# Attention steps of a two-block kernel: the weighing of values and the next projection's products regrouped by two

## The reference, cut to what matters

```
sc = einsum("bnqhd,bknjhd->bhnqkj", q_r, k_r) * scale
sc = where(mask, sc + bias, NEG)
p  = softmax(sc)
o  = einsum("bhnqkj,bknjhd->bnqhd", p, v_r)
```

## Time and profile before

| what | value |
|---|---|
| median of 3 runs | 2443.91 us |
| the 3 runs | 2440.36, 2443.91, 2445.88 us |
| the profiled execution's own time | 2440.27 us |
| its span in the profile | 2438.4 us |
| granted clock of PE, mean | 0.997 |
| PE busy | 2409.4 us, 99% |
| DVE, POOL, ACT busy | 77%, 56%, 38% |
| chain that ended last | PE 86%, DVE 7%, POOL, ACT and issue 2% each |
| PE busy from 1190 to 1440 us, where the pairs lie | 248.78 of 250 us |

### The profile page before, as it was taken

The page is one execution under the profiler, slowest core; times in us unless marked ns, Lnnn a source line. Parts: engine busy times, 40 slices in busy tenths (PEclk is TensorE's granted clock), DMA queues, the critical chain, the costliest instruction groups (busy, mean ns, idle before and its releaser), DMA issues.

```text
span 2438.4 us, 37303 instructions
## 1 busy us (share of the span) xinstructions
PE 2409.4 (99%) x13817; PEld 1978.4 (81%) x13817; DVE 1875.5 (77%) x1904; ACT 937.0 (38%) x1288; POOL 1361.0 (56%) x789
## 2 busy tenths in 40 slices
PE   8999999999999999999999999999999999999998
PEld 8788887888888788887777778888888888887886
DVE  6755555776666788888877789354799999999998
ACT  5333335353333533314233331310355445443433
POOL 3322222269887767772322223333379999978785
PEclk9999999999999999999999999999999999999999
DMA  6111112334444755431311111113222222235342
GB/s 226 36 37 41 34 34 92 108 119 151 153 155 166 262 167 160 150 125 39 127 41 33 40 35 52 44 48 126 95 87 78 86 91 81 77 132 179 104 122 81
DMA packets 243637, 244.79 MB, mean 100 GB/s; under 512 B 16944, under 2 KB 212187, under 8 KB 238811
## 3 DMA queue, kind: packets, MB, share of 16 engines
q1 hardware_dynamic: 214484, 165.13, 21.9%
q10 hardware_dynamic: 29062, 78.44, 8.4%
HBM read 181.13 MB, written 64.17 MB: 101 GB/s over the span
## 4 chain that ended last, share of the span: by engine, by line
PE 86%; DVE 7%; POOL 2%; issue 2%; ACT 2%; DMA 1%; SPq 0%; DVEq 0%; ACTq 0%; POOLq 0%
PE psum L1414 30%; PE psum L1703 26%; PE psum L1823 11%; PE psum L2069 7%; PE psum L1972 3%; PE psum L1452 2%; PE psum L1538 1%; PE psum L1904 1%; PE psum L1477 1%; PE psum L1885 1%; DVE sq_sum_gain L3474 0%; POOL ffn_s_lo L1283 0%; PE psum L1598 0%; DVE h_lo L2949 0%; DVE sq_sum L3231 0%
## 5 line engine op out<-in xcount | busy, mean ns | idle before, releaser
L1226 POOL CAST w_hi<-w_raw 128x1024 fp32r<-128x1024 f32 x85 | 100.4, 1181 | 773.8 <-issue 375.2
L1414 PE MATMUL psum<-h_hi,w_hi 128*128 128x512 f32 x1040 | 333.4, 402 | 1.5 <-DVE h_lo L3052 1.3
L1414 PE MATMUL psum<-h_lo,w_hi 128*128 128x512 f32 x1040 | 321.9, 391 | 0.0
L1414 PE MATMUL psum<-h_hi,w_lo 128*128 128x512 f32 x1040 | 320.8, 390 | 0.0
L1414 PEld LDWEIGHTS psum<-h_hi,w_lo 128*128 128x128 f32 x1040 | 195.5, 188 | 42.0
L1414 PEld LDWEIGHTS psum<-h_lo,w_hi 128*128 128x128 f32 x1040 | 195.5, 188 | 41.7
L1234 POOL TENSOR_TENSOR w_lo<-w_raw,w_hi 128x1024 fp32r<-128x1024 f32 x85 | 222.7, 2620 | 9.9 <-DVE h_lo L2949 3.2
L1414 PEld LDWEIGHTS psum<-h_hi,w_hi 128*128 128x128 f32 x1040 | 189.5, 188 | 42.9 <-issue 7.3
L3528 DVE SCALAR_TENSOR_TENSOR conv_t<-u_t,cols,conv_t 128x1024 f32<-128x1024 f32 x120 | 179.8, 1498 | 2.4
L1283 POOL TENSOR_TENSOR ffn_s_lo<-ffn_s_sum,ffn_s_hi 128x512 fp32r<-128x512 f32 x84 | 159.8, 1932 | 7.0 <-POOL ffn_s_sum L1269 4.1
L1703 PE MATMUL psum<-ffn_t_hi,ffn_s_hi 128*128 128x512 f32 x252 | 98.0, 389 | 0.0
(11 more groups left out here) (605 smaller groups left out, 6808.3 us busy)
## 6 DMA issues: line engine op xcount, KB each, us to landing
w_raw<-in_w_in SPq DMA_DIRECT2D x120, 256.0 KB, 3.0
w_raw<-in_w_up SPq DMA_DIRECT2D x76, 256.0 KB, 3.4
act_parts<-act_mixed ACTq DMA_DIRECT2D x15, 1024.0 KB, 3.8
down_part_raw<-act_parts SPq DMA_DIRECT2D x14, 1024.0 KB, 5.4
down_part_raw<-act_parts SPq DMA_DIRECT2D x15, 768.0 KB, 6.4
ffn_raw<-in_w_up SPq DMA_DIRECT2D x44, 256.0 KB, 3.4
ffn_rows<-ffn_gate ACTq DMA_DIRECT2D x22, 512.0 KB, 2.6
ffn_part_raw<-ffn_rows SPq DMA_DIRECT2D x18, 512.0 KB, 4.7
```

Source lines behind the costliest of these rows:

```text
L1226: pool.tensor_copy(hi, raw).then_inc(weight_hi, 1)
L1414: last = pe.matmul(psum[:, first_bank + t, :], w, a[:, k, t * HALF:(t + 1) * HALF], start=(k == order[0] and j == 0), stop=(k == order[-1] ...
```

## The change

The fourth projection's feature tiles no longer follow steps 1 to 8 one by one. Two of them, P(k) and P(k+1), stand together in each of the steps 2, 4, 6 and 8. The weighing of values is done in every other step, for two groups: step 4 has W(0) and W(1), step 6 W(2) and W(3), step 8 W(4) and W(5), step 10 W(6) and W(7). The steps 1, 3, 5, 7 have S(g) and T(g-1) alone, and step 1 also Tv. The wait for `v_tiles_ready` moves from step 3 to step 4. Since the transposed weights of two groups are now held while a third is copied, `prob_t` gets a third buffer of 3 KB a partition (`prob_t_third`, behind `u_t` in the arena), and the index is `g % 3`. Nothing is computed otherwise, and the number of matmuls, copies and transfers is the same.

```diff
-NEXT_AFTER = {k + 1: [k] for k in range(KT)}
+NEXT_AFTER = {k + 2: [k, k + 1] for k in range(0, KT, 2)}
...
+            ("prob_t_third", [P, 2, WIN], F32))
+        prob_t_slots = [prob_t[:, 0, :, :], prob_t[:, 1, :, :], prob_t_third[:, :, :]]
...
                         pe.matmul(psum[head, g // 4, (g % 4) * P:(g % 4 + 1) * P], v_keys[:, first + c, head],
-                                  prob_t[:, g % 2, j, c * P:(c + 1) * P], start=(c == 0), stop=(c == n - 1))
+                                  prob_t_slots[g % 3][:, j, c * P:(c + 1) * P], start=(c == 0), stop=(c == n - 1))
...
                 for g in range(1, GROUPS + 3):
-                    if g == 3:
+                    if g == 4:
                         pe.wait_ge(v_tiles_ready, p + 1)
-                    if g >= 3:
+                    if g >= 4 and g % 2 == 0:
+                        weigh_values(p, g - 4)
                         weigh_values(p, g - 3)
...
-                        act.activation(prob_t[:, g % 2, j, 0:n], psum[:, 6 + j, 0:n], ACT.Copy).then_inc(prob_t_ready, 1)
+                        act.activation(prob_t_slots[g % 3][:, j, 0:n], psum[:, 6 + j, 0:n], ACT.Copy).then_inc(prob_t_ready, 1)
```

More of the change, by code:

```diff
@@ L502, in two_blocks @@
         U_PAD = CONV_PAD + SEQ + CONV_PAD
-        (sig_cb, q_hi, q_lo, k_hi, k_lo, v_t, v_keys, bias_raw, prob_t, bias, near_mask, prob, qk32, u_t) = arena(
+        (sig_cb, q_hi, q_lo, k_hi, k_lo, v_t, v_keys, bias_raw, prob_t, bias, near_mask, prob, qk32, u_t,
+         prob_t_third) = arena(
             ("sig_cb", [P, CT, SEQ], F32), ("q_hi", [P, SEQ], F32R), ("q_lo", [P, SEQ], F32R),
@@ L508, in two_blocks @@
             ("bias", [P, 2, 5, P], F32), ("near_mask", [P, 3, P], F32), ("prob", [P, 2, 2, WIN], F32),
-            ("qk32", [P, SEQ], F32), ("u_t", [P, 2, U_PAD], F32))
+            ("qk32", [P, SEQ], F32), ("u_t", [P, 2, U_PAD], F32),
+            ("prob_t_third", [P, 2, WIN], F32))
+        prob_t_slots = [prob_t[:, 0, :, :], prob_t[:, 1, :, :], prob_t_third[:, :, :]]
         inv_spread, inv_wide = qk32, v_t
```

## The result

The changed kernel takes 2445.93 us in the median of 22 runs (2443.17 to 2447.72), the kernel before 2440.97 in the median of 22 (2438.51 to 2445.88). The medians lie 4.96 us apart. The ratio put on record is 1.0015, with a 95% interval of 1.0009 to 1.0021: 3.7 us slower (2.2 to 5.1), where +4.2 was forecast. The forecast's 2448.1 stands 2.2 us too high, since it was built on a median of three runs that lay 2.9 us above that of 22.

What follows compares the result with a forecast made beforehand. PE, busy nearly throughout, was taken as the bound; per pair 0.73 us of blocks plus 0.32 of waits gave 1.05, over four pairs 4.2, added to 2443.91 for 2448.1 us; range 2442.0 to 2452.5.

Steps and rivals of the forecast that it cites:

- The cover: Steps 1 and 2: T(1) starts as before, about 1.2 us idle replaces P(0), whose 1.36 us must be done later.
- P: Behind T(1), seven lone product blocks (10.85 us) become four double ones of 2.91 (11.64): +0.79 us a pair.
- W: Behind T(1), seven weighing blocks become four, each block saved worth 0.14 us: -0.42 us a pair.
- T ahead of W: Steps 4, 6, 8: transposes now followed by weighing cost 0.12 us more each, bounds 0 to 0.14: +0.36 a pair.
- T on ACT: Even steps, waits for ACT's copies: T(5) free by 0.26 us, T(3) none or 0.02, T(7) 0.3.
- The sum: Over a pair, 0.73 us of blocks plus 0.32 of waits: 1.05 us, four pairs 4.2 us slower.
- some 9 us of listed waits: In the pairs, PE's waits were to rise from 1.2 us to some 9.
- Rival 1: Even steps: ACT's copies land some 0.3 us later, about 0.6 more a pair, 6.6 in all, 2450.5 us; chance 0.26.
- Rivals 2 to 4: In the pairs: T(1) earlier, 2442.3 us, or everything hidden (0.10 together); passages costing more than block lengths show, 2438.3 us (0.04).
- the signs of being wrong: In the changed profile: T(1) moves up, T(3) or T(5) wait 0.2 us or more, or a double P under 2.8.
- the 0.2% that I had called no change: Whole kernel: a measurement tells about 0.2%, 4.9 us, from no change; chance of same 0.59, slower 0.36, faster 0.05.

Runs made afterwards that it cites:

- e1: The change with P(0) back alone in step 1 and P(1) alone in step 2; pairs 224.55 us, ratio 1.0005.
- e2: The change with products still paired in even steps but values weighed one group a step as before; median 2453.59 us, ratio 1.0053.
- e3: The change with values still weighed for two groups but products one a step as before; pairs 223.77 us, ratio 1.0003.
- e4: Against the change: products one a step, values weighed two groups at once in steps 5 and 7, singly in 3, 8, 9, 10; ratio 0.9994.
- e5: The change with DVE's convolution tap after group 0 taken to the end of the pair; pairs 223.27 us, ratio 0.9995.
- e6: The order of the kernel before, with the third buffer, DVE's tap after group 0 at the pair's end; pairs 221.74 us, ratio 0.9992.
- e7: The change with both regroupings one step earlier, paired products in steps 3, 5, 7 and paired values in 5, 7, 9; pairs 220.57 us, ratio 0.9983.
- e8: e7 with DVE's tap after group 0 taken to the end of the pair; median 2440.65 us, ratio 0.9995.
- e9: e8 with the four pairs' taps counted 21, 21, 20, 20 in place of 20, 20, 22, 20; median 2436.99 us, ratio 0.9982.
- e10: The same file as e7, timed again together with e9; pairs 220.50 us, ratio 0.9992.

## Why the prediction was right

All at once, the pairs against those of before (us); expected from block lengths, measured in one profile each:

| kernel | expected | measured | ratio |
|---|---|---|---|
| the change | +4.2 | +4.78 | 1.0015 |
| e1, P(0) back | +1.4 | +1.49 | 1.0005 |
| e2, products alone | +12 | +12.16 | 1.0053 |
| e3, values alone | +0.8 | +0.71 | 1.0003 |
| e4, values in odd steps | -1.1 | -0.97 | 0.9994 |
| e5, change, tap later | 0.0 | +0.21 | 0.9995 |
| e6, before, tap later | -1.4 | -1.32 | 0.9992 |
| e7, both odd | -1.8 | -2.49 | 0.9983 |
| e8, both odd, tap later | -3.2 or -1.8 | +0.14 | 0.9995 |
| e9, e8 with even taps | -3.8 | -3.85 | 0.9982 |
| e10, e7 again | -2.5 | -2.56 | 0.9992 |

- **The cover.** T(1) stayed at 4.75 us behind S(1), and the idle time appeared where P(0) was: 0.26 ahead of Tv and, of the 1.2 foretold ahead of S(2), 1.05 as listed and 1.17 start to start. e1 and e5 show the cause from both ends: with P(0) back the loss shrinks, with DVE's tap gone it does too.
- **P.** 2.94 for a double one, 2.91 was reckoned: 11.75 us a pair for four, and not 11.64. The seven lone ones of before were read too short as well, 10.91 in all and not 10.85, so the term is +0.84 in place of +0.79.
- **W.** 1.46 for 24, as reckoned; the term is -0.45 in place of -0.42.
- **T ahead of W.** 0.80 or 0.81 against 0.63, so 0.18 and not the 0.12 taken from Tv, and above my upper bound of 0.14: another +0.17 a pair. The bound was wrong because I read the passage's price from other pairs of neighbours. That it costs at all agrees with the Trainium skill's sentence on drains at a change of tiling mode (TensorEngine Tiling (Array Packing), Key Properties).
- **T on ACT.** T(3) and T(5) did not wait, as forecast. T(7) lost 0.20 us (0.07 and 0.13) in three pairs where I had 0.3; the later T, by its dearer passages, met a copy that was nearer. In the fourth pair it lost 0.56: DVE began the scores of group 7 1.16 us behind S(7) (1426.48 to 1427.64) and not 0.81. It does so in the kernel before as well (1420.80 to 1421.96), where P(6) stood ahead of T(7) and hid it; I had read the first pair only. Why DVE is later there was not tried.
- **The sum.** 1.12 us from T(1) to the block of 20 in three pairs, 1.05 forecast: 0.84 for P, -0.45 for W, 0.53 for T ahead of W and 0.20 of waits. The passage was 0.17 too cheap and the waits 0.12 too dear, so part of the nearness is luck. The fourth pair, 1.44, was not foreseen. The list of waits was off more: I foretold some 9 us of listed waits, the profile lists 5.8, since the one ahead of Tv and the short ones of T(7) are not in it and S(2) of the second pair waits only 0.58.
- **The rivals.** Rival 1 (ACT late in all even steps) did not come in the change, but e2 is what it looks like when one W less stands there. Rivals 2 to 4 would have needed T(1) to move or blocks to be worth more; neither was seen. Of the signs of being wrong (T(1) earlier, T(3) or T(5) late by 0.2, a double P below 2.8) none came.
- **The level.** +0.15% fell inside the 0.2% that I had called no change, as forecast, and was told from zero only by 22 runs a side.

## What to carry to other kernels

Work of a busy engine that stands in front of a point set by other engines is free there, as long as it fits in, and costs its full length anywhere else; before moving it, check whether the next wait would come at the same time without it. Regrouping saves the passages between kinds of work, here 0.14 us for a W block and 0.2 for a P block; it pays only in an order that keeps each distance from a producer to its consumer (here 3.4 us from S(g) to T(g)) filled, and shifting the grouping by one step, with P(0), P(1), W(0) and W(7) left single, turned +4.8 us into -2.5. After that, look for the engine whose list sets the point itself: moving one tap of DVE was worth 4.6 us in the change and 1.3 in the order of before, and 1.3 on top of e7 once DVE's list had room for it (e9); without that room it lost 2.6 (e8).

## What was not expected of the hardware

- A passage has a price that depends on both neighbours: eight transposes take 0.85 us ahead of a 128x128 product and 0.97 ahead of a 64x128 one (in e6 too, where DVE's maximum for S(2) is there 1.29 us early, so that it is no hidden wait), six take 0.63 ahead of a product and 0.81 ahead of a 128x64 one.
- A wait of PE of 2.34 us was followed, 1.6 us after its end, by some 3.5 us at the lower clock (granted 0.60 from 1398 to 1402 us) and 1.55 us more went there than in the other pairs. In the changed kernel waits of 1.05 us, three times, and of 0.58 once did nothing of the kind: the granted clock is 1.00 over the six microseconds that hold each of them and what follows it.
- DVE's tap of 128x1024 takes 1.2 us start to start, but some that lie beside POOL's `w_lo` take far longer: one of 3.42 us at 1388.32 in the kernel before, 0.07 behind the start of a `w_lo` of 2.40 us, and at the end of the third pair four took 5.86 us in e6 and 7.87 in e8. What decides which is hit was not tried. POOL's own operation took 2.39 us in one place and 3.25 in another.
